# Halving the first load of a ten-stage fp32 kernel and splitting its last two projection blocks by tokens

## The chip, the cores and the metric

The kernel runs on one core of one Trainium2 chip. The metric is the device time of one execution in microseconds (us), the median over the runs shown. A core has five engines that work side by side, each through its own list of instructions in order: TensorE (PE, matrix products), VectorE (DVE), ScalarE (ACT), GpSimd (POOL) and SyncE (SP, which here only issues transfers). They wait for one another by semaphores. Transfers between the large memory (HBM) and the on-chip memory are issued by SP or by POOL, and all of them run on the core's 16 DMA engines.

## What is computed

Two models in a row on one sequence `x` of 256 tokens with 1024 features, all in float32. The first has two layers, each a mixer of three attention kinds (block attention, compressed and windowed attention, gated linear attention) followed by a feed-forward layer with a short convolution. The second has two layers, each with a feed-forward layer, a mixer (a short convolution in the first, a gated delta rule in the second) and another feed-forward layer. The end of the second model is what matters for the last part of the change:

```python
def second_block(x, norm_g, ...):
    h = x
    for i in range(DEPTH):
        g = norm_g[i]
        ff = swiglu(rms_norm_2(h, g[0]), ffn_w_gate_up[i, 0], ffn_w_down[i, 0])
        h = h + 0.5 * rms_norm_2(ff, g[1])
        ...
        ff = swiglu(rms_norm_2(h, g[4]), ffn_w_gate_up[i, 1], ffn_w_down[i, 1])
        h = h + 0.5 * rms_norm_2(ff, g[5])
    return h

def swiglu(x, w_gate_up, w_down):
    gate, up = jnp.split(x @ w_gate_up, 2, axis=-1)
    return (jax.nn.silu(gate) * up) @ w_down
```

So the last thing computed is a product with `w_down`, its norm over the 1024 features of each token, a gain, and the sum with `h`.

## The kernel before

**Stages.** `stage_list` gives ten stages: HYBRID, FFN1, HYBRID, FFN1, then FFN2, SHORT, FFN2, FFN2, DELTA, FFN2. `x` stays on the chip for the whole run, as `x[128, 2, 1024]`: 128 partitions, two chunks of 128 tokens, 1024 features. Its four quarters of 512 columns (`quarter(q)`: chunk `q % 2`, column half `q // 2`) are what a stage updates.

**Weights.** All weights come as panels of 128 x 1024 floats (512 KB), one per step, in the order of use, into a ring of six buffers `raw` (`RING = 6`). A product of float32 numbers is made of three products of rounded parts (`mm3`). So each panel is split on the chip: ACT writes the rounded part `whi` (`hi`, L991), DVE the rest `wlo = raw - whi` (`lo`, L1537), and PE waits for `lo_done`. SP reloads a ring buffer when `lo_done` says that it has been read.

**Start.** SP issues the masks, the whole of `x`, the column constants `cols` and the first six panels. PE runs ten products of a matrix of ones (L2969) and then waits for `x`. `turn_x` transposes `x` in eight tiles of 128 features and five groups (`TURNS = ((0,), (1,), (2, 3), (4, 5), (6, 7))`) into PSUM; ACT scales each tile and writes `xhi` (L1007), DVE writes `xlo` (L1548). ACT puts the split of panel 0 behind tile 1, and DVE does the same. Then `up` (L2321) multiplies panel 0, and so on. ACT also squares `x` for the norm.

**POOL at the start.** It waits for the masks and for the whole of `x` (L869), and then issues the setup loads of the hybrid stage: six constants (L882) and four small weights, `w1_in` (2 MB), `w2_in`, `pos_in` and `gate_w_in` (L887), counted by `small_loaded`. PE waits for the six before the small table product at L2491, ahead of tile 3.

**DVE's order at the start.** It is written out by hand: splits of panels and reads of tiles take turns. After its read of tile 1 DVE waits for `small_loaded` (L1823) and copies the tile into the input of the compression (L1827, L1829). Behind that in its list is the split of panel 5.

**End.** In the last stage (FFN2) each block of 128 hidden features has two `up` panels and one `down` panel. `down` (L2373) adds `h.T @ w_down` into four banks, one for each quarter, for all 256 tokens; it runs two blocks behind (`LAG = 2`), so two `down` blocks stand at the end. `finish` on ACT (L1021) squares the four banks with a running sum per token as each is complete, then takes one root for both chunks. `finish` on DVE (L1563) multiplies each bank by the gain (L1576), adds the two column halves' sums (L1573), takes the reciprocal (L1579) and makes four updates `x = gained * rstd + x` (L1591). SP waits for all four and stores `x` with one transfer of 1 MB (L857 to L859).

Of the kernel before, what the change touches and what calls it, by code (L numbers as in the profile page):

```python
# [4 lines left out]
P = 128  # L5
D = 1024
S = 256
KT = D // P
# [293 lines left out]
def build(nc, stages, arrays):  # L302
# [14 lines left out]
    with ExitStack() as ctx:  # L317
# [7 lines left out]
        HALF = D // 2  # L325
        QUARTERS = 2 * CHUNKS

        def quarter(q):
# [203 lines left out]
        def mixed(k):  # L532
# [16 lines left out]
            "consts table_product table stored rel_loaded small_loaded tile_read tok_read "  # L549
            "gla_gained squared qk_ms qk_root qk_scaled qk_turned nsa_ready moba_ready gains low_tanh gsum cmp_x "  # L550
            "cmp_hidden cmp_bias cmp_act cmp_kv vc_copied o_cmp s_sum t_ready p_ready p_scaled gated "
# [9 lines left out]
            "l16_sum l16 l32_sum l32 t32 l64_sum l64 new_sum new v1_in o_sum o_copied o_squared o_added o_root o_inv o_scaled o_turned").split()}  # L561
        x_loaded = sem("x_loaded")
        cols_loaded = sem("cols_loaded")
        landed = [sem(f"landed{i}") for i in range(RING)]
# [123 lines left out]
        def wait_x(eng, s, q):  # L688

            if s == 0:  # L690
                eng.wait_ge(x_loaded, 16)
            else:
                eng.wait_ge(x_updated, QUARTERS * (s - 1) + q + 1)

# [83 lines left out]
        def _(sp):  # L778
            sp.dma_start(masks[:], masks_in).then_inc(masks_loaded, 16)
            sp.dma_start(x[:], x_in).then_inc(x_loaded, 16)  # L780
            sp.dma_start(cols[:], cols_in).then_inc(cols_loaded, 16)
            for j in range(RING):
                sp.dma_start(raw[j][:], panels[j]).then_inc(landed[j], 16)
# [72 lines left out]

            sp.wait_ge(x_updated, QUARTERS * n_stages)  # L857
            sp.dma_start(out, x[:]).then_inc(stored, 16)
            sp.wait_ge(stored, 16)  # L859


        @block.gpsimd
        def _(pool):
# [4 lines left out]
            pool.wait_ge(masks_loaded, 16)  # L868
            pool.wait_ge(x_loaded, 16)  # L869
            def hybrid(s):  # L870
# [110 lines left out]
        def _(act):  # L981
# [16 lines left out]
            def prepare(s):  # L998

                for k in range(KT):  # L1000
                    g, src = turned(s, k)
                    if k == TURNS[g][0]:
                        act.wait_ge(x_turned, len(TURNS) * s + g + 1)
                    if s == 0 and k == 2:

                        hi_to(0)
                    act.activation(xhi[:, k, :], src, ACT.Copy, scale=col(("pre", s), k)).then_inc(xhi_ready, 1)  # L1007
                hi_to(1)
                if posts_before(s):
                    act.wait_ge(post_squared, QUARTERS * posts_before(s))  # L1010
                for c in range(CHUNKS):
                    wait_x(act, s, QUARTERS - CHUNKS + c if s and post_norm(s - 1) else QUARTERS - 1)
                    if s or c:
                        act.wait_ge(sum_ready, CHUNKS * s + c)
                    act.activation(psq[:, :, :].rearrange("p a b -> p (a b)"), x[:, c, :], ACT.Square,
                                   accum_out=row_sums[:, c:c + 1]).then_inc(sum_ready, 1)
                act.wait_ge(sum_ready, CHUNKS * (s + 1))
                act.activation(row_root[:], row_sums[:], ACT.Sqrt, scale=1.0 / D, bias=eps_col[:, 0:1]) \
                    .then_inc(root_ready, 1)

            def finish(s):  # L1021

                act.activation(root_of_one[:, s:s + 1], ones[:, 0:1], ACT.Sqrt)
                if not post_norm(s):
                    return
                n = posts_before(s)
                for q in range(QUARTERS):
                    wait_acc(act, s, q)
                    if q >= 2:
                        act.wait_ge(post_squared, QUARTERS * n + q - 1)  # L1030
                    act.activation(psq[:, q % 2, :], bank[q][:], ACT.Square, accum_out=post_parts[:, q:q + 1]) \
                        .then_inc(post_squared, 1)
                act.wait_ge(post_sum_ready, n + 1)
                half = 4.0 if stages[s][0] == FFN2 else 1.0
                act.activation(post_root[:], post_sum[:], ACT.Sqrt, scale=half / D,
                               bias=eps_col[:, 1:2] if half == 4.0 else eps_col[:, 0:1]).then_inc(post_root_ready, 1)
                hi_to(down_panel(s, n_blocks(s) - 1) + LEAD + 1)
# [60 lines left out]
            def hybrid(s):  # L1098
# [19 lines left out]
                def nsa_heads_ready():  # L1118

                    v("qk_turned", 0, 2)  # L1120
                    v("gains", 1, 2)
                    for i in range(4):
                        last = act.activation(qkn[:, i, :], bank[2 + i // 2][:, i % 2 * S:(i % 2 + 1) * S], ACT.Copy,
                                              scale=qk_gain[:, i:i + 1])
                    last.then_inc(y["nsa_ready"], 1)
# [397 lines left out]
        def _(dve):  # L1523
# [33 lines left out]
            def copy_rstd(s):  # L1557
# [3 lines left out]
                dve.wait_ge(rstd_ready, s + 1)  # L1561

            def finish(s):  # L1563
                n = posts_before(s)
                if post_norm(s):
# [160 lines left out]
            def hybrid(s):  # L1726
# [5 lines left out]
                def start():  # L1732

                    if n == 0:
                        link(dve.tensor_reduce(quarters[:], ident.rearrange("p (g j) -> p j g", g=4), AX.X, ALU.add))
                    g = col_at[("qk_gain", s)]
                    dve.tensor_copy(qk_gain[:], cols[:, g:g + 8]).then_inc(y["gains"], 1)
                    v("gains", 0, 2)
                    dve.tensor_scalar(qk_gain[:, 2:6], cols[:, g + 2:g + 6], -(HD ** -0.5), None, ALU.mult) \
                        .then_inc(y["gains"], 1)  # L1740

                    dve.tensor_scalar(gla_gain[:], col(("gla_gain", s)), 0.5, None, ALU.mult) \
                        .then_inc(y["gla_gained"], 1)

# [93 lines left out]
                def step(k):  # L1838
# [10 lines left out]
                    if k == 1:  # L1849
                        v("cmp_hidden", 1, 2)  # L1850
                        dve.tensor_copy(cmp_small[:, 0:1], bank[7][:, NCMP:NCMP + 1]).then_inc(y["cmp_bias"], 1)
                        v("gains", 1, 2)
                        v("qk_turned", 1, 2)
# [117 lines left out]
                    if k == OUT_SLOT + 3:  # L1971
                        v("gla_gained", 0, 1)
                        v("sgate", 0, 1)
# [324 lines left out]
            for k in range(KT):  # L2298
                if k == 2:
                    lo_to(0)  # L2300
                prepare_tile(0, k)
# [12 lines left out]
        def _(pe):  # L2314
# [24 lines left out]
            def turn_x(s):  # L2339
# [9 lines left out]
                for g, ks in enumerate(TURNS):  # L2349
# [9 lines left out]
                    for k in ks:  # L2359
                        dst = turned(s, k)[1]  # L2360
                        for c in range(CHUNKS):
                            last = pe.transpose(dst[:, c * P:(c + 1) * P], x[:, c, k * P:(k + 1) * P], ident)  # L2362
                    last.then_inc(x_turned, 1)

            def spread_rstd(s):
# [7 lines left out]
            def down(s, f, p, turn):  # L2373
# [5 lines left out]
                for q in range(QUARTERS):  # L2379
# [4 lines left out]
                    if q < QUARTERS - 1 and ends:  # L2384

                        last.then_inc(acc_ready, 1)
                last.then_inc(panel_used, 1)

            def blocks_of(s):
                kind = stages[s][0]  # L2390
                def body(f, turn):
# [31 lines left out]
                    if f >= LAG:  # L2423
                        down(s, f - LAG, down_panel(s, f - LAG), turn)
                run_blocks(pe, s, body)
                for f in range(n_blocks(s) - LAG, n_blocks(s)):
                    down(s, f, down_panel(s, f), None)
# [567 lines left out]
```

## Time and profile before

| | us |
|---|---|
| median of 3 runs | 1993.9 |
| the three runs | 1993.9, 1994.35, 1991.03 |
| span of the profiled execution (first to last instruction) | 1991.5 |
| PE busy | 1961.4 (98%) |
| DVE busy | 1398.7 (70%) |
| ACT busy | 1095.4 (55%) |
| POOL busy | 125.0 (6%) |
| mean DMA throughput | 175 GB/s |
| mean granted clock of PE, share of full | 0.995 |

The profiled execution has no time of its own beside its span; the runs' median lies 2.4 us above that span. A busy share is the share of the span in which the engine had an instruction under way. Matrix products overlap, so the distance between two starts says more than the duration of one. An idle time in brackets stands with what ended it.

### The profile page before, as it was taken

To read this page: it belongs to the slowest core of one execution; us is meant where nothing else is said; L and a number is where in the kernel's file an instruction comes from. 1 tells how busy PE (TensorE), PEld (TensorE's weight loads), DVE (VectorE), ACT (ScalarE), POOL (GpSimd) and SP (SyncE) were. 2 spreads that over 40 slices of the span, in tenths; PEclk is the share of its full clock that TensorE was granted. 3 is DMA by queue.
4 is the path that set the end of the run, shared out by engine and by line. 5 is a ranking of instruction groups with operands and counts; after the bars stand their busy time and mean duration, and the time that the engine had idled before them with its cause. 6 is when DMAs were issued, how large, how long until landed. Compare 5 with 4: busy or idle time off the path is not lost.

```text
span 1991.5 us, 41716 instructions
## 1 busy us (share of the span) xinstructions
PE 1961.4 (98%) x15682; PEld 1827.6 (92%) x15682; DVE 1398.7 (70%) x2392; ACT 1095.4 (55%) x1828; POOL 125.0 (6%) x204
## 2 busy tenths in 40 slices
PE   9999999999999999999999999999999899999998
PEld 7999999989999999999999999999999899989997
DVE  6687877766788877666667766666658977577655
ACT  5665555556654655554454544454447777565443
POOL 2031000000040000000000000000000432000000
PEclk9999999999999999999999999999999899999999
DMA  9433665554335555465546465555554535455552
GB/s 319 143 128 128 217 210 189 187 170 149 128 118 190 200 187 186 156 212 189 190 159 212 151 202 187 189 174 187 188 190 150 164 123 155 149 173 195 188 187 82
DMA packets 117817, 348.51 MB, mean 175 GB/s; under 512 B 23288, under 2 KB 35912, under 8 KB 117184
## 3 DMA queue, kind: packets, MB, share of 16 engines
q1 hardware_dynamic: 114960, 335.23, 50.6%
q0 software_dynamic: 2736, 11.59, 1.7%
q8 instruction: 85, 1.39, 0.3%
q14 instruction: 36, 0.29, 0.1%
HBM read 340.81 MB, written 5.96 MB: 174 GB/s over the span
## 4 chain that ended last, share of the span: by engine, by line
PE 90%; DVE 4%; ACT 2%; issue 1%; DMA 1%; POOL 1%; SPq 0%; DVEq 0%; ACTq 0%; POOLq 0%
PE bank L2317 28%; PE bank L2319 27%; PE bank L2318 27%; PE bank L2609 1%; ACT whi L991 1%; DVE arena L1576 1%; DVE wlo L1537 1%; DVE conv L2038 1%; PE bank L2353 1%; PE bank L2582 0%; DMA relay<-arena 0%; PE bank L2796 0%; PE bank L2570 0%; PE bank L2362 0%; DVE xlo L1548 0%
## 5 line engine op out<-in xcount | busy, mean ns | idle before, releaser
L2317 PE MATMUL bank<-xhi,whi 128*128 128x256 f32 x3368 | 958.4, 285 | 7.3 <-DVE arena L2031 2.6
L2318 PE MATMUL bank<-xlo,whi 128*128 128x256 f32 x3368 | 943.9, 280 | 1.1 <-issue 1.1
L2319 PE MATMUL bank<-xhi,wlo 128*128 128x256 f32 x3368 | 943.2, 280 | 1.1 <-issue 1.1
L1537 DVE TENSOR_TENSOR wlo<-raw,whi 128x1024 fp32r<-128x1024 f32 x621 | 750.1, 1230 | 199.6 <-ACT whi L991 196.9
L2317 PEld LDWEIGHTS bank<-xhi,whi 128*128 128x128 f32 x3368 | 635.7, 189 | 24.3 <-issue 6.1
L2318 PEld LDWEIGHTS bank<-xlo,whi 128*128 128x128 f32 x3368 | 636.2, 189 | 5.8
L991 ACT ACTIVATE whi<-raw 128x1024 fp32r<-128x1024 f32 x621 | 632.2, 1045 | 11.9 <-DMA raw<-panels 6.2
L2319 PEld LDWEIGHTS bank<-xhi,wlo 128*128 128x128 f32 x3368 | 635.8, 189 | 1.2 <-issue 1.2
L2317 PE MATMUL bank<-whi,hhi 128*128 128x512 f32 x688 | 272.8, 396 | 0.0
L2319 PE MATMUL bank<-whi,hlo 128*128 128x512 f32 x688 | 271.2, 394 | 0.0
L2318 PE MATMUL bank<-wlo,hhi 128*128 128x512 f32 x688 | 270.4, 393 | 0.0
L1048 ACT ACTIVATE act_out<-first 128x256 f32<-128x256 f32 x89 | 37.3, 419 | 301.9 <-DVE first L1662 301.7
L1662 DVE TENSOR_TENSOR first<-bank,rstd 128x256 f32<-128x256 f32 x132 | 56.0, 424 | 184.8 <-PE bank L2319 184.6
L1070 ACT ACTIVATE hhi<-h 128x256 fp32r<-128x256 f32 x172 | 71.9, 418 | 185.5 <-PE bank L2319 125.6
L2319 PEld LDWEIGHTS bank<-whi,hlo 128*128 128x128 f32 x688 | 129.4, 188 | 29.9
L2318 PEld LDWEIGHTS bank<-wlo,hhi 128*128 128x128 f32 x688 | 130.1, 189 | 23.5
L2317 PEld LDWEIGHTS bank<-whi,hhi 128*128 128x128 f32 x688 | 129.3, 188 | 23.4
L1055 ACT ACTIVATE conv<-first,cols 128x256 f32<-128x256 f32 x44 | 26.5, 603 | 126.6 <-DVE first L1662 126.6
L1699 DVE TENSOR_TENSOR hlo<-h,hhi 128x256 fp32r<-128x256 f32 x172 | 71.9, 418 | 24.0 <-ACT hhi L1070 19.3
L1693 DVE TENSOR_TENSOR h<-act_out,second 128x256 f32<-128x256 f32 x132 | 55.8, 423 | 22.3 <-ACT act_out L1061 22.3
L1161 ACT ACTIVATE arena<-arena 128x256 f32<-128x256 f32 x48 | 20.0, 417 | 70.2 <-DVE arena L1819 70.2
L932 POOL DMA_DIRECT2D arena<-gains_in x6 | 3.3, 550 | 850.4 <-DVE arena L1576 721.3
(376 smaller groups left out, 1751.8 us busy)
## 6 DMA issues: line engine op xcount, KB each, us to landing
raw<-panels SPq DMA_DIRECT2D x621, 512.0 KB, 3.8
arena<-w_in POOLq DMA_DIRECT2D x2, 2048.0 KB, 10.5
arena<-relay SPq DMA_DIRECT2D x8, 512.0 KB, 5.0
arena<-gains_in POOLq DMA_DIRECT2D x6, 512.0 KB, 3.9
relay<-arena POOLq DMA_DIRECT2D x4, 512.0 KB, 9.1
relay<-arena SPq DMA_DIRECT2D x4, 512.0 KB, 3.6
x<-x_in SPq DMA_DIRECT2D x1, 1024.0 KB, 5.0
arena<-bias_table POOLq DMA_DIRECT2D x8, 128.0 KB, 6.5
```

The source lines that it names most:

```text
L991: act.activation(whi[slot][:], raw[slot][:], ACT.Copy).then_inc(hi_done, 1)
L1048: act.activation(act_out[:, sl, :], first[:, sl, 2:], ACT.Silu).then_inc(act_done, 1)
L1055: act.activation(conv[:, sl, :], first[:, sl, 2:], ACT.Identity, scale=tap(s, 2, f, turn), bias=conv_bias(s, f, turn)) \
L1070: act.activation(hhi[:, sl, :], h[:, sl, :], ACT.Copy).then_inc(hhi_done, 1)
L1161: act.activation(g, g, ACT.Tanh, scale=0.5).then_inc(y["merged"], 1)
L1537: dve.tensor_tensor(wlo[slot][:], raw[slot][:], whi[slot][:].bitcast(F32), ALU.subtract) \
L1662: dve.tensor_tensor(first[:, sl, 2:], pair[:, 0:S], rstd[:], ALU.mult).then_inc(gate_scaled, 1)
L1693: dve.tensor_tensor(h[:, sl, :], gated, second[:, sl, :], ALU.mult).then_inc(h_done, 1)
L1699: dve.tensor_tensor(hlo[:, sl, :], h[:, sl, :], hhi[:, sl, :].bitcast(F32), ALU.subtract) \
L2317: pe.matmul(dst, w_hi, a_hi, start=start, stop=False, skip_group_check=True)
L2318: pe.matmul(dst, w_hi, a_lo, start=False, stop=False, skip_group_check=True)
L2319: return pe.matmul(dst, w_lo, a_hi, start=False, stop=stop, skip_group_check=True)
```

## The change

It has five parts.

1. `x` is loaded in two halves of 512 columns: masks, first half, `cols`, panel 0, second half, panels 1 to 5. Whoever needs tiles 0 to 3 waits for the first half, everyone else, POOL's first wait among them, for the second.
2. In the first stage PE issues products of ones between the groups of transposes: 1, 1, 6, 2 and 2 of them behind the five groups.
3. ACT and DVE split panel 0 behind tile 3 in place of tile 1.
4. The last two `down` blocks of the last stage are done first for tokens 0 to 127 and then for tokens 128 to 255. The banks are complete in the order 0, 2, 1, 3. Square, sum, root, reciprocal and update are done for each chunk of tokens by itself, and each quarter of `x` is stored by a transfer of its own.
5. The semaphore `gla_gained` is merged into `gains`, whose count per hybrid stage goes from 2 to 3.

```diff
+        LAST_ORDER = (0, 2, 1, 3)
...
+        x_second_half_loaded = sem("x_second_half_loaded")
...
         def wait_x(eng, s, q):
             if s == 0:
-                eng.wait_ge(x_loaded, 16)
+                eng.wait_ge(x_loaded if q < CHUNKS else x_second_half_loaded, 16)
...
         def _(sp):
             sp.dma_start(masks[:], masks_in).then_inc(masks_loaded, 16)
-            sp.dma_start(x[:], x_in).then_inc(x_loaded, 16)
+            sp.dma_start(x[:, :, 0:HALF], x_in[:, :, 0:HALF]).then_inc(x_loaded, 16)
             sp.dma_start(cols[:], cols_in).then_inc(cols_loaded, 16)
-            for j in range(RING):
+            sp.dma_start(raw[0][:], panels[0]).then_inc(landed[0], 16)
+            sp.dma_start(x[:, :, HALF:], x_in[:, :, HALF:]).then_inc(x_second_half_loaded, 16)
+            for j in range(1, RING):
                 sp.dma_start(raw[j][:], panels[j]).then_inc(landed[j], 16)
...
-            sp.wait_ge(x_updated, QUARTERS * n_stages)
-            sp.dma_start(out, x[:]).then_inc(stored, 16)
-            sp.wait_ge(stored, 16)
+            for i, q in enumerate(LAST_ORDER):
+                c, j = quarter(q)
+                sp.wait_ge(x_updated, QUARTERS * (n_stages - 1) + i + 1)
+                sp.dma_start(out[:, c, j * HALF:(j + 1) * HALF], x_quarter(q)).then_inc(stored, 16)
+            sp.wait_ge(stored, 16 * QUARTERS)
...
             pool.wait_ge(masks_loaded, 16)
-            pool.wait_ge(x_loaded, 16)
+            pool.wait_ge(x_second_half_loaded, 16)
...
-                    if s == 0 and k == 2:
+                    if s == 0 and k == KT // 2:
                         hi_to(0)
...
+                if s == n_stages - 1:
+                    for i, q in enumerate(LAST_ORDER):
+                        wait_acc(act, s, i)
+                        if i >= 2:
+                            act.wait_ge(post_squared, QUARTERS * n + i - 1)
+                        act.activation(psq[:, i % 2, :], bank[q][:], ACT.Square, accum_out=post_parts[:, q:q + 1]) \
+                            .then_inc(post_squared, 1)
+                        if i % 2:
+                            c = i // 2
+                            act.wait_ge(post_sum_ready, n + 1 + c)
+                            act.activation(post_root[:, c:c + 1], post_sum[:, c:c + 1], ACT.Sqrt, scale=4.0 / D,
+                                           bias=eps_col[:, 1:2]).then_inc(post_root_ready, 1)
+                    return
...
+            def finish_last(s):
+                n = posts_before(s)
+
+                def weighted(i):
+                    q = LAST_ORDER[i]
+                    dve.wait_ge(post_squared, QUARTERS * n + i + 1)
+                    dve.tensor_tensor(gained[:, q, :], bank[q][:], gain[:, q // CHUNKS * HALF:(q // CHUNKS + 1) * HALF],
+                                      ALU.mult).then_inc(post_gained, 1)
+
+                dve.wait_ge(gain_loaded, 16 * (n + 1))
+                for c in range(CHUNKS):
+                    cs = slice(c, c + 1)
+                    weighted(2 * c)
+                    dve.wait_ge(post_squared, QUARTERS * n + 2 * c + 2)
+                    dve.tensor_tensor(post_sum[:, cs], post_parts[:, cs], post_parts[:, CHUNKS + c:CHUNKS + c + 1], ALU.add) \
+                        .then_inc(post_sum_ready, 1)
+                    weighted(2 * c + 1)
+                    dve.wait_ge(post_root_ready, n + 1 + c)
+                    dve.reciprocal(post_rstd[:, cs], post_root[:, cs]).then_inc(post_rstd_ready, 1)
+                    dve.wait_ge(post_rstd_ready, 3 * n + 1 + c)
+                    for i in (2 * c, 2 * c + 1):
+                        q = LAST_ORDER[i]
+                        dve.wait_ge(post_gained, QUARTERS * n + i + 1)
+                        dve.scalar_tensor_tensor(out=x_quarter(q), in0=gained[:, q, :], scalar=post_rstd[:, cs],
+                                                 in1=x_quarter(q), op0=ALU.mult, op1=ALU.add).then_inc(x_updated, 1)
...
-                if k == 2:
+                if k == KT // 2:
                     lo_to(0)
                 prepare_tile(0, k)
...
                     last.then_inc(x_turned, 1)
+                    if s == 0:
+                        for i in range(6 if ks[-1] == KT // 2 - 1 else len(ks)):
+                            pe.matmul(bank[2][:, 0:P], ones[:], ones[:], start=True, stop=True)
...
+            def last_downs(s):
+
+                nb = n_blocks(s)
+                for c in range(CHUNKS):
+                    ts = slice(c * P, (c + 1) * P)
+                    for f in (nb - 2, nb - 1):
+                        p = down_panel(s, f)
+                        slot, sl = p % RING, f % 2
+                        pe.wait_ge(lo_done, used(p))
+                        pe.wait_ge(hlo_done, first_block[s] + f + 1)
+                        for j in range(2):
+                            q, cs = CHUNKS * j + c, slice(j * HALF, (j + 1) * HALF)
+                            last = mm3(bank[q][:], hhi[:, sl, ts], hlo[:, sl, ts], whi[slot][:, cs], wlo[slot][:, cs],
+                                       False, f == nb - 1)
+                            if f == nb - 1 and q != LAST_ORDER[-1]:
+                                last.then_inc(acc_ready, 1)
+                        if c == CHUNKS - 1:
+                            last.then_inc(panel_used, 1)
...
                 run_blocks(pe, s, body)
+                if s == n_stages - 1:
+                    last_downs(s)
+                    return
                 for f in range(n_blocks(s) - LAG, n_blocks(s)):
                     down(s, f, down_panel(s, f), None)
```

## Rows read from the trace of the kernel before

**Rows 1.** The page: PE's busy time, and the chain that ended last.
```profile
PE 1961.4 (98%) x15682; PEld 1827.6 (92%) x15682; DVE 1398.7 (70%) x2392; ACT 1095.4 (55%) x1828; POOL 125.0 (6%) x204
...
PE 90%; DVE 4%; ACT 2%; issue 1%; DMA 1%; POOL 1%; SPq 0%; DVEq 0%; ACTq 0%; POOLq 0%
```

**Rows 2.** Timeline, first 12 us: start, duration, engine and line, operation, [idle before].
```profile
6.32 1.94 PE L2362 MATMUL bank<-masks,x 128*128 128x128 f32 x16 [1.04 <-DMA x<-x_in]
...
6.83 0.67 POOL L882 DMA_DIRECT2D rel_table<-rel_in  x1 [5.76 <-DMA x<-x_in]
...
8.15 1.06 ACT L991 ACTIVATE whi<-raw 128x1024 fp32r<-128x1024 f32 x1 [0.48 <-DMA raw<-panels]
...
10.52 0.39 PE L2317 MATMUL bank<-xhi,whi 128*128 128x256 f32 x1 [2.27 <-DVE wlo L1537]
...
11.74 0.52 POOL L887 DMA_DIRECT2D arena<-gate_w_in  x1
```

**Rows 3.** DMA issues up to 34 us: size, and us from issue to landing.
```profile
arena<-w_in POOLq DMA_DIRECT2D x1, 2048.0 KB, 12.9
x<-x_in SPq DMA_DIRECT2D x1, 1024.0 KB, 5.0
...
arena<-gate_w_in POOLq DMA_DIRECT2D x1, 16.0 KB, 13.8
```

**Rows 4.** Timeline of DVE, 25 to 28 us.
```profile
25.57 0.66 DVE L1827 COPY arena<-tmp 128x240 f32<-128x240 f32 x2 [4.74 <-DMA arena<-gate_w_in]
...
26.23 1.22 DVE L1537 TENSOR_TENSOR wlo<-raw,whi 128x1024 fp32r<-128x1024 f32 x1
```

**Rows 5.** Timeline of PE's weight loads, 27.2 to 28 us: the first of panel 5.
```profile
27.50 0.19 PEld L2317 LDWEIGHTS bank<-whi,xhi 128*128 128x128 f32 x1 [0.23 <-DVE wlo L1537]
```

**Rows 6.** Timeline of all engines, from 1977 us to the end.
```profile
1977.82 0.43 DVE L1699 TENSOR_TENSOR hlo<-h,hhi 128x256 fp32r<-128x256 f32 x1 [1.85 <-ACT hhi L1070]
...
1979.91 0.39 PE L2317 MATMUL bank<-whi,hhi 128*128 128x512 f32 x1
...
1981.59 2.02 DVE L1576 TENSOR_TENSOR arena<-bank,arena 128x512 f32<-128x512 f32 x3 [3.34 <-ACT psq L1031]
...
1982.46 0.39 PE L2319 MATMUL bank<-whi,hlo 128*128 128x512 f32 x1
...
1982.89 0.60 ACT L1031 ACTIVATE psq<-bank 128x512 f32<-128x512 f32 x1
...
1983.61 0.16 DVE L1573 TENSOR_TENSOR post_sum<-post_parts 128x2 f32<-128x2 f32 x1
...
1983.81 0.30 ACT L1035 ACTIVATE post_root<-post_sum,eps_col 128x2 f32<-128x2 f32 x1 [0.23 <-DVE post_sum L1573]
1984.29 0.16 DVE L1579 RECIPROCAL post_rstd<-post_root 128x2 f32<-128x2 f32 x1
1984.48 2.74 DVE L1591 SCALAR_TENSOR_TENSOR x<-arena,post_rstd,x 128x512 f32<-128x512 f32 x4
1987.25 0.34 SPq L858 DMA_DIRECT2D out<-x  x1
```

**Rows 7.** DMA issues at the end, and all panel loads up to 40 us.
```profile
out<-x SPq DMA_DIRECT2D x1, 1024.0 KB, 3.9
...
DMA to landing us min/median/max: 3.2/8.5/12.0
```

**Rows 8.** Three windows: busy (x count) of PE, PEld, DVE, ACT, POOL; granted clock; DMA share; GB/s.
```profile
12.00:15.00 3.00, 3.00 (x17) 3.00 (x16) 1.98 (x5) 2.88 (x7) 1.25 (x3) 0.52 1.02 406
1568.00:1572.00 4.00, 0.22 (x2) 0.01 (x1) 3.96 (x12) 3.93 (x10) 0.00 (x0) 0.92 0.72 200
1572.00:1582.00 10.00, 9.63 (x251) 9.05 (x252) 8.31 (x19) 6.00 (x9) 0.00 (x0) 0.52 0.71 237
```

**Rows 9.** DMA queues, 16 to 22 us and 22 to 25 us (q0: POOL's, q1: SP's).
```profile
q0 software_dynamic: 144, 2.03, 80.1%
...
q1 hardware_dynamic: 281, 1.02, 87.8%
```

More of the change, by code:

```diff
@@ L549, in build @@
             "consts table_product table stored rel_loaded small_loaded tile_read tok_read "
-            "gla_gained squared qk_ms qk_root qk_scaled qk_turned nsa_ready moba_ready gains low_tanh gsum cmp_x "
+            "squared qk_ms qk_root qk_scaled qk_turned nsa_ready moba_ready gains low_tanh gsum cmp_x "
             "cmp_hidden cmp_bias cmp_act cmp_kv vc_copied o_cmp s_sum t_ready p_ready p_scaled gated "
@@ L1011, in prepare @@
                 for c in range(CHUNKS):
+                    if s == 0:
+                        wait_x(act, s, 0)
                     wait_x(act, s, QUARTERS - CHUNKS + c if s and post_norm(s - 1) else QUARTERS - 1)
@@ L1120, in nsa_heads_ready @@
                     v("qk_turned", 0, 2)
-                    v("gains", 1, 2)
+                    v("gains", 1, 3)
                     for i in range(4):
@@ L1561, in copy_rstd @@
                 dve.wait_ge(rstd_ready, s + 1)
+            def finish_last(s):
[21 more added lines that the diff above has]
+                                                 in1=x_quarter(q), op0=ALU.mult, op1=ALU.add).then_inc(x_updated, 1)
             def finish(s):
+                if s == n_stages - 1:
+                    finish_last(s)
+                    return
                 n = posts_before(s)
@@ L1737, in start @@
                     dve.tensor_copy(qk_gain[:], cols[:, g:g + 8]).then_inc(y["gains"], 1)
-                    v("gains", 0, 2)
+                    v("gains", 0, 3)
                     dve.tensor_scalar(qk_gain[:, 2:6], cols[:, g + 2:g + 6], -(HD ** -0.5), None, ALU.mult) \
@@ L1742, in start @@
                     dve.tensor_scalar(gla_gain[:], col(("gla_gain", s)), 0.5, None, ALU.mult) \
-                        .then_inc(y["gla_gained"], 1)
+                        .then_inc(y["gains"], 1)
                 def heads_mean(i, at, n_heads):
@@ L1851, in step @@
                         dve.tensor_copy(cmp_small[:, 0:1], bank[7][:, NCMP:NCMP + 1]).then_inc(y["cmp_bias"], 1)
-                        v("gains", 1, 2)
+                        v("gains", 1, 3)
                         v("qk_turned", 1, 2)
@@ L1971, in step @@
                     if k == OUT_SLOT + 3:
-                        v("gla_gained", 0, 1)
+                        v("gains", 2, 3)
                         v("sgate", 0, 1)
@@ L2363, in turn_x @@
                     last.then_inc(x_turned, 1)
+                    if s == 0:
+                        for i in range(6 if ks[-1] == KT // 2 - 1 else len(ks)):
+                            pe.matmul(bank[2][:, 0:P], ones[:], ones[:], start=True, stop=True)
             def spread_rstd(s):
@@ L2425, in blocks_of @@
                 run_blocks(pe, s, body)
+                if s == n_stages - 1:
+                    last_downs(s)
+                    return
                 for f in range(n_blocks(s) - LAG, n_blocks(s)):
```

## The prediction

> **What bounds the kernel now.** I read the page first: TensorE (PE) is busy for 98% of the span [rows 1], so almost everything is one queue of products, and a change moves the time only where PE waits, or before its first and after its last product. So I read next the timeline of the first 12 us, the DMA landings and waits up to 34 us, and the timeline from 1977 us on.
>
> In the front [rows 2] the reader is to see that the transposes start at 6.32, when the whole input has landed (issued at 1.22, 5.0 us to landing [rows 3]), and that the first product starts at 10.52, after ACT and DVE have split panel 0 (its load landed by 8.15). But the front does not end there. VectorE (DVE) sits idle 4.74 us ahead of L1827, until 25.57, for four small-weight loads of the GpSimd queue (`small_loaded`) [rows 4]. The last is `gate_w_in`, issued at 11.74 and landed 13.8 us later, at 25.54 [rows 2, 3]. Behind this wait on DVE's queue stands the split of panel 5 (26.23 to 27.45) [rows 4], and PE's first weight load of panel 5 starts at 27.50, released by that very split [rows 5]. So **two paths meet at 27.5**: PE's own work, and GpSimd's load, then DVE. PE had stalled there for at most 0.2 us.
>
> At the end [rows 6], PE's last block is 12 products, 1979.91 to 1982.46, 0.232 us apart, the last one done at 1982.85. Then come: the square (1982.89, 0.70 with its read), the sum (1983.61), the root (1983.81 to 1984.11), the reciprocal (1984.29), four updates (1984.48 to 1987.22), and one 1 MB store, issued at 1987.25 and landed 3.9 us later at 1991.15 [rows 7]. That is 8.3 us behind PE's last product, with everything in series.
>
> **The front, part by part.** (a) Halving the input. The SP queue's loads land in the order of issue: masks, input, columns, panels. The first half then has 0.5 MB fewer bytes ahead of its end; at 0.41 MB per us, the rate of 12 to 15 us [rows 8], it lands about 1.2 us earlier, near 5.0. The transposes of tiles 0 to 3 can follow the ten warm-up products at once (these end at 5.27, the 1.04 us before 6.32), ScalarE can begin near 5.7 and is free for panel 0, which lands near 6.9, when it has scaled four tiles. I put panel 0's split ready at about 10.1 in place of 10.5: 0.4 us. (b) The 12 added ones products cost 0.22 us each at full clock (two passes of 128 columns), some 2.7 us; eight stand between the first three turns and the second half's arrival, where PE would wait in any case, the other four in the 2.27 us that PE now idles before 10.52 [rows 2]. Cost nothing; if that cover is gone, 0.9 us. What they can give: from 12 to 15 us the granted clock is 0.52 of full [rows 8], the 1.2 GHz level, after that idle time; full clock there is worth about 1.6 us. So PE would arrive at panel 5 about 2.0 us earlier. (c) One more SP issue (0.42 us) is ahead of panels 1 to 5 and delays none that is awaited. (d) **GpSimd's wait moves.** It stood on the whole input, at 6.2; it now stands on the second half, which is issued behind panel 0. The bytes ahead of its end are those ahead of panel 0's end now, so it lands near 8.1: 1.9 us later. Queued behind the wait are all ten setup loads, `gate_w_in` last. Are they shifted one for one? The first was issued at 6.83 [rows 2]. While `w1_in` moves, the GpSimd queue has 80% of the DMA engines' time; in 22 to 25, when the last small ones move, SP's queue has 88% [rows 9]. SP's panels keep a backlog throughout: what it moves early in those 1.9 us it has fewer later, but 5.2 MB for panels 1 to 10 at 0.41 MB per us, with GpSimd's 2.9 MB (2 MB of them `w1_in` [rows 3]) beside it, fill the engines until about 27.5. So no hole opens for the shifted loads to catch up in. I take 1.9 us; the ends are 0 (they catch up wholly) and 2.2.
>
> So `small_loaded` comes at 27.4, DVE's two copies and panel 5's split end at 29.35 (the same 1.9 us as from 25.54 to 27.45), and PE starts panel 5 at 29.4 in place of 27.5. The 2.0 us that (a) and (b) give are spent waiting there: **the front loses 1.9 us.** The small-table product at L2491 waits for the first six loads, at 17.0 now, 18.9 then, when PE reaches it at about 19.2: nothing. POOL's table store follows panel 5 and is not near a bound.
>
> (e) PE then idles from about 25.6 to 29.4. After 2.27 us idle it was granted half clock at 12 to 15; after the 4 us around 1568 to 1572 (busy 0.22) the next 10 us were at 0.52 [rows 8]. So I expect half clock again on panels 5 and 6. In the first case it began about 3.2 us after the idle time did and lasted to about 14.8; put from 25.6 on, it lies over 29.4 to 31.9 and costs half of that, 1.2 us. The ends are 0 and 4.8 (the 10 us stretch). The Trainium skill (TensorE: Matmul & The Clock Gate, Part 1) says that an idle array falls back to 1.2 GHz; by that rule, the trace agrees.
>
> After panel 5 PE is the bound: the chain that ended last lies on it for 90% [rows 1], and the squares and turns that follow start from panel 5's end. The shift passes to the end one for one. The merge of `gla_gained` into `gains` changes no order of work: nothing.
>
> **The tail.** `last_downs` has the same 24 products, in another order. Its block 20 begins near 1977.1 (12 products ahead of 1979.91) and has six products for tokens 0 to 127, so needed at 1978.5 is `hlo` of the last block, ready at 1978.25 [rows 6]: cover 0.25 us; if it is gone, the difference is lost. Bank 0 is whole at 1979.4, bank 2 at 1980.1, bank 1 at 1982.15, bank 3 at 1982.85 as now. For tokens 0 to 127: squares 1979.4 to 1980.8; gain products of 0.68 [rows 6] from 1980.2; sum by 1981.05; root by 1981.4; reciprocal 1981.8; two updates of 0.685, to 1983.2. All this lies beside PE or after it. DVE is now the bound for the other tokens: gain product of bank 1 to 1983.9, sum 1984.05, gain product of bank 3 to 1984.65 (the root, 1984.1 to 1984.4, beside it), reciprocal 1984.8, updates to 1985.5 and 1986.2. In place of 1987.22: **1.0 us.** Late next is DVE's queue, as the sum waits 0.3 us for it.
>
> The last store has 256 KB in place of 1 MB; three go before it, 0.7 us apart or more, so they have drained. The price of such a store is in no row: below stands 3.9 less the 0.79 MB that it has fewer, at 0.41 MB per us, 2.0; above, the fastest 512 KB panel load, 3.2 [rows 7]. I take 2.3, near the first because that is the same kind of transfer: 1.6 us saved, between 0.7 and 1.9. [...] **The tail gains 2.6 us.**
>
> **Sum:** 1.9 + 1.2 - 2.6 = +0.5 us on the profiled execution, 1991.5 to 1992.0. The median of the three runs is 1993.9, 2.4 above that span, so the forecast is 1994.4 us. A measurement of this kernel can tell about 0.2%, 4 us, from no change; the three runs lie 3.3 us apart.
>
> **Rivals.** A (forecast, chance 0.5): as above. B, the GpSimd loads catch up (0.2): DVE's wait ends at 25.5 as now, the front neither gains nor loses, the tail gives 2.6: 1991.3. For it: in 16 to 22 its queue has 80% of the DMA time, so it is hardly slowed by SP. Against it: the last small loads crawl beside SP's 88% [rows 9]. C, DVE's wait is no gate and PE's lead survives (0.1): -2.0 - 2.6 gives 1989.3. Against it is the load at 27.50, released by the split [rows 5]. D, the slower side (0.1): the idle time ahead of panel 5 brings the long half-clock stretch, as after 1572. Its place is panels 5 to 8, its price 4.8 in place of 1.2, and it decides if the stretch outlasts panel 6: 1998.0. E, the tail gives nearly nothing (0.1): PE stalls in `last_downs` by the lost cover, and the store costs 3.2: 1994.4 + 1.2, 1995.6. The change not doing what it says would be that the ones products do not hold the clock in the first two tiles: nothing in the time under A, since PE waits at panel 5.
>
> **How the numbers follow.** The likeliest is A's 1994.4. The range takes in B, E and D's edge, with the spread of the three runs about A: 1990.4 to 1997.9. Faster by over 0.2% means below 1989.9: most of C and the edge of B, 0.09. Slower means above 1997.9: half of D and the edge of A, 0.08. The rest is 0.83.
>
> **What would show it.** GpSimd's first setup load issued near 8.7; L1827 on DVE near 27.4 after over 6 us idle; PE's wait ahead of panel 5 of 3 us or more, with half clock after it; the last update ending 3.4 us after PE's last product, in place of 4.4; the last store landing about 2.3 us after its issue. L1827 at 25.6 would make (d) wrong; a start of panel 5 before 27.5 would make the whole front wrong.

## The result, and the profile after

The changed kernel takes **1996.12 us** in the median of 21 runs (1991.76 to 2000.4), the kernel before 1993.57 us in 21 runs beside it (1989.88 to 1996.29). The ratio is 1.0015, 95% interval [1.0009, 1.0021]: about 3 us slower, inside the 0.2% that the prediction called no change, and inside its range. The profile is of the fastest of the 21 runs: its span is 1990.0 us, 1.5 *under* that of the profile before. So the profile alone would say the opposite of the median, and what lies between them became the question of the experiments.

PE's line of the page, which answers to [rows 1]:

```profile
PE 1963.5 (99%) x15706; PEld 1829.0 (92%) x15706; DVE 1398.2 (70%) x2394; ACT 1096.2 (55%) x1829; POOL 124.6 (6%) x204
```

PE has 24 products and 24 weight loads more: the twelve products of ones, two passes each. The 48 matter further down.

**The front.** Timeline of the changed kernel, answering to [rows 2] and [rows 4] (L2412 is the transposes, L2417 the added ones, L888 GpSimd's first setup load, L1877 DVE's copy behind the small weights, L1558 the splits):

```profile
6.04 0.41 PE L2412 MATMUL bank<-masks,x 128*128 128x128 f32 x2 [0.34 <-DMA x<-x_in]
...
10.04 0.63 PE L2412 MATMUL bank<-masks,x 128*128 128x128 f32 x4 [1.15 <-DMA x<-x_in]
...
10.54 0.68 POOL L888 DMA_DIRECT2D rel_table<-rel_in  x1 [9.47 <-DMA x<-x_in]
...
13.07 0.39 PE L2367 MATMUL bank<-xhi,whi 128*128 128x256 f32 x1 [1.07 <-DVE wlo L1558]
...
27.09 0.66 DVE L1877 COPY arena<-tmp 128x240 f32<-128x240 f32 x2 [4.59 <-DMA arena<-gate_w_in]
...
27.75 1.22 DVE L1558 TENSOR_TENSOR wlo<-raw,whi 128x1024 fp32r<-128x1024 f32 x1
...
29.02 0.50 PE L2367 MATMUL bank<-whi,xhi 128*128 128x512 f32 x1 [0.31 <-DVE wlo L1558]
```

The first half of `x` lands at 6.0, hardly before the whole did (6.2), as it took 4.7 us from its issue and the whole 5.0; the second lands at 9.9. The first product starts at 13.07 in place of 10.52. The first two of the following rows are DMA issues of the changed kernel (both halves with their median, then the second half alone); the two behind them are the window from 2 to 4 us, of the kernel after and before, whose last column is GB/s:

```profile
x<-x_in SPq DMA_DIRECT2D x2, 512.0 KB, 5.8
...
x<-x_in SPq DMA_DIRECT2D x1, 512.0 KB, 6.8
...
2.00:4.00 2.00, 2.00 (x11) 2.00 (x11) 0.00 (x0) 0.25 (x2) 0.00 (x0) 1.00 0.61 170
```

```profile
2.00:4.00 2.00, 2.00 (x11) 2.00 (x11) 0.00 (x0) 0.24 (x2) 0.00 (x0) 1.00 0.99 304
```

From 2 to 4 us the 16 DMA engines are busy for 61% in place of 99% and move 170 GB/s in place of 304. All the traces of this document divide so: in the seven with the halved load the rate is 155 to 190 GB/s, in the seven with the whole one 297 to 319. The half of `x` goes as 256 rows of 2 KB in place of 128 of 8 KB, and its issue occupies SP for 0.69 us in place of 0.42. Some 0.27 MB are lost there, and everything behind is late. For all that, `gate_w_in` lands only 1.5 us later than before (11.6 us after an issue at 15.47, in place of 13.8 after 11.74), and PE starts panel 5 at 29.02 in place of 27.5. PE does not wait at panel 5 for long (0.31 us, its weight load 0.75), as it comes late itself. There is no half clock in the front: behind the warm-up products the granted clock is 1.00 up to 1572 us.

**The end**, answering to [rows 6] and [rows 7]:

```profile
1983.99 0.40 PE L2369 MATMUL bank<-whi,hlo 128*128 128x512 f32 x1
...
1984.54 0.68 DVE L1590 TENSOR_TENSOR arena<-bank,arena 128x512 f32<-128x512 f32 x1
...
1985.15 0.16 DVE L1598 TENSOR_TENSOR post_sum<-post_parts 128x1 f32<-128x1 f32 x1
1985.22 0.68 DVE L1590 TENSOR_TENSOR arena<-bank,arena 128x512 f32<-128x512 f32 x1
...
1985.82 0.15 DVE L1602 RECIPROCAL post_rstd<-post_root 128x1 f32<-128x1 f32 x1
1986.01 1.41 DVE L1607 SCALAR_TENSOR_TENSOR x<-arena,post_rstd,x 128x512 f32<-128x512 f32 x2
...
out<-x SPq DMA_DIRECT2D x4, 256.0 KB, 2.1
```

DVE is never idle here for longer than 0.1 us. The last update ends 3.0 us behind PE's last product (4.4 before), and a store of 256 KB lands in 2.1 us.

**Between front and end.** ACT runs one small root at the end of each of the ten stages, so that line splits the span. Before (L1023) and after (L1031):

```profile
L1023 ACT ACTIVATE root_of_one<-ones x10: 186/203/203, 235.4 to 1979.1; 128x1 f32<-128x1 f32 x10
```

```profile
L1031 ACT ACTIVATE root_of_one<-ones x10: 188/203/205, 236.9 to 1980.6; 128x1 f32<-128x1 f32 x10
```

The first stage is 1.5 us longer, the piece behind the last root 3.1 shorter (12.4 and 9.3), and all the others agree within 0.1 us in this pair. (Over all fourteen profiles of this document, every stage but the first and the ninth agrees within 0.2 us.) The ninth, the delta stage, hides something. It lies from 1504 to 1791 us here. PE's waits in it that no semaphore explains, which the profile puts down to "issue", are, in the window 1640 to 1680 us, before and after:

```profile
PE bank L2319 <- issue: 1.1, 1, 1.1
```

```profile
PE bank L2902 <- issue: 3.6, 1, 3.6
```

and its timeline after:

```profile
1655.77 0.68 PE L2902 MATMUL bank<-arena 32*16 32x16 f32 x59
1660.03 0.21 PE L2902 MATMUL bank<-arena 32*16 32x16 f32 x3 [3.59 <-issue]
```

PE stands for 3.6 us three products short of the end of a run of small ones (32 rows, 16 columns, two operations of the list for each product), which it works off at about 11 ns each. I counted PE's operations (weight loads, products, its own waits) from 5 us ahead of the stage: the long wait falls at operation 3839, and a shorter one at 2559. Before, waits of 1.1 us fall at 3887 and 2607, and one of 1.6 at 4911, for which the changed kernel has no counterpart. The two in each kernel lie 1280 apart, five times 256 (the third another 1024, four times 256), and the pairs lie 48 apart: the 48 operations that the products of ones add in front. The page's queue q8, "instruction", moved 1.39 MB in 85 transfers, 16 KB each. From this came theory F: PE's list is fetched in blocks of 256, and a block whose end falls in a run of very short products, or right behind one, is awaited longest. The Trainium skill (Runtime: NRT & Kernel Launch, Terms) has the engines' instruction memory refilled in blocks of 16 KiB, and (Perfetto Trace Analysis, The 4-stage abstract model) an instruction of 64 bytes; 16 KiB by 64 bytes is 256, an estimate from both, and the traces agree.

### The profile page after: what moved, and what is told of

It is laid out like the page before. It is cut to its first block, busy times and chain, and to the rows that moved or that the text cites. A ratio compares the mean times of both kernels' runs of the same rounds, so it can differ in the third digit from the quotient of the medians.

```text
span 1990.0 us, 41775 instructions
## 1 busy us (share of the span) xinstructions
PE 1963.5 (99%) x15706; PEld 1829.0 (92%) x15706; DVE 1398.2 (70%) x2394; ACT 1096.2 (55%) x1829; POOL 124.6 (6%) x204
## 3 DMA queue, kind: packets, MB, share of 16 engines
q8 instruction: 85, 1.39, 0.3%
## 4 chain that ended last, share of the span: by engine, by line
PE 91%; DVE 3%; ACT 2%; DMA 2%; POOL 1%; issue 1%; SPq 0%; DVEq 0%; ACTq 0%; POOLq 0%
PE bank L2367 28%; PE bank L2369 27%; PE bank L2368 27%; PE bank L2685 1%; ACT whi L997 1%; DVE arena L1626 1%; DVE wlo L1558 1%; DMA arena<-gate_w_in 1%; PE bank L2403 1%; PE bank L2872 0%; PE bank L2658 0%; PE bank L2646 0%; PE bank L2412 0%; POOL arena L978 0%; DVE xlo L1569 0%
## 5 line engine op out<-in xcount | busy, mean ns | idle before, releaser
L1558 DVE TENSOR_TENSOR wlo<-raw,whi 128x1024 fp32r<-128x1024 f32 x621 | 749.8, 1230 | 201.1 <-ACT whi L997 198.4
```

Of the source, the lines that this page charges most:

```text
L1558: dve.tensor_tensor(wlo[slot][:], raw[slot][:], whi[slot][:].bitcast(F32), ALU.subtract) \
```

## The experiments

Times are medians; each ratio is to the kernel before, run beside it. A change of 0.001 is 2 us. The three numbers behind a run are, from its profile, the first stage, the delta stage and the piece behind the last root (before: 235.4, 287.4 and 12.4 us; after: 236.9, 287.3 and 9.3).

**The end alone**, everything else as before:

> The kernel before with the change's end alone: last two down blocks by token halves, norm per half, four stores. Theory G (the end gains, the front loses through GpSimd's late setup loads): 3.0 us faster than the kernel before, as the profile after shows 5.6 us from PE's last product to the end of the span in place of 8.6; the front as before (DVE's wait for small_loaded ends near 25.5). Rival T (the end is what made the change slower, by a wait that the one profile does not show): no gain or a loss.

Measured: 1988.5 us, ratio 0.9981 [0.9971, 0.9991]; 235.5, 287.8, 9.3. And once more, with other kernels beside it:

> The end alone once more, beside the variants of this call: 3.1 us under the kernel before by the length of the last piece of the span (9.3 in place of 12.4 us), and not the 3.8 of the first measurement of nine runs.

Measured: 1989.27 us, 0.9984 [0.9975, 0.9993]; 235.5, 286.0, 9.3. The end gives its 3 us; rival T falls.

The second profile also shows the gate at panel 5 [rows 5] at work. Its granted clock was 1.00 from 12 to 16 us, with no added products, where the kernel before has 0.64. So PE came to panel 5 earlier, its weight load waited 0.89 us there in place of 0.23, and the first stage was no shorter:

```profile
27.57 0.19 PEld L2363 LDWEIGHTS bank<-whi,xhi 128*128 128x128 f32 x1 [0.89 <-DVE wlo L1554]
```

**The front alone** (the end undone):

> The change with its end undone: halved load, ones products, panel 0 split later, GpSimd's wait on the second half. Theory G: slower than the kernel before by 2.6 + 3.0 = 5 to 6 us, which the front of the profile after (1.5 us) shows only in part; this profile should show DVE's wait for small_loaded ending later than 27.1, or half clock behind PE's idle time ahead of panel 5. Rival T: within 1 us of the kernel before.

Measured: 1998.18 us, 1.0026 [1.0015, 1.0036]; 237.9, 287.1, 12.4. It costs 5 us, of which this profile, again of one of the fastest runs, shows half, in the first stage. T falls a second time. DVE's wait ended at 28.0, and PE's weight load waited 1.89 us for panel 5, in place of 0.75 in the profile of the change with the same front:

```profile
29.92 0.19 PEld L2349 LDWEIGHTS bank<-whi,xhi 128*128 128x128 f32 x1 [1.89 <-DVE wlo L1543]
```

So what GpSimd's moved wait costs differs from run to run.

**GpSimd waits for the first half:**

```diff
-            pool.wait_ge(x_second_half_loaded, 16)
+            pool.wait_ge(x_loaded, 16)
```

> The change, but GpSimd waits for the first half of x only, so its ten setup loads are issued from about 6.6 us on, as in the kernel before. Theory G: DVE's wait for small_loaded ends near 25.5 again and the time falls by what the front lost: 3 to 5 us under the change, 1 to 3 us under the kernel before. Rival L (the slow loads of 2 KB rows and PE's late start at panel 0, 13.1 in place of 10.5, are the loss, and GpSimd's wait is not): no different from the change.

Measured: 1994.2 us, 1.0007 [0.9999, 1.0016]; 236.4, 290.2, 9.3. DVE's wait ended at 25.3, as theory G has it, and the first stage is 0.5 us shorter: the moved wait is real, but by these profiles a small part. The median is some 1.5 us under the change, with intervals that overlap; G's 3 to 5 us are not there.

**The change again:**

> The changed kernel itself, for a second profile, since the first is of the fastest of its 21 runs. Theory G: 2 to 3 us over the kernel before in the median; in the profile the first stage is longer than the 236.9 us of the first profile, by 2 to 4 us, and all the stages between as before. Rival N (nothing in the front; the spread lies in a later stage): stage one at 236.9 and a later stage longer.

Measured: 1995.91 us, 1.0012 [1.0003, 1.0021]; 236.7, 292.4, 9.3. The first stage is as in the first profile; **the delta stage is 5 us longer.** That is rival N. The stalls are at 2559 and 3839 again, 2.1 and 3.6 us, with a third of 1.1 us at 1535, and the clock is at half from 1574 for 6.8 us, from 1615 for 6.8 and from 1663 for 6.8; in the change's first profile it was from 1572 for 10.2 and from 1661 for 3.4. Theory F was formed here.

**Forty-eight operations and nothing else**, in the kernel before:

```diff
             for i in range(10):
                 pe.matmul(bank[2][:, 0:P], ones[:], ones[:], start=True, stop=True)
+            for i in range(12):
+                pe.matmul(bank[2][:, 0:8], ones[:], ones[:, 0:8], start=True, stop=True)
             pe.wait_ge(masks_loaded, 16)
```

> The kernel before with twelve more products of ones, 8 columns each, behind the ten warm-up products, where PE waits 1.0 us for x. They add 48 instructions to PE's list, as the change's twelve do, and nothing else. Theory F (PE's instructions are fetched in blocks of 256; 48 more in front move a block's end into the delta rule's run of small products, and PE stands there without instructions): the delta stage shows the long stall at instruction 3839 of the stage, 3.6 us in place of 1.1 at 3887, as all four traces of the changed front do, and the time is 2 to 5 us over the kernel before, with a front longer by at most 0.5 us. Rival G (the loss is the late loads in the front): no stall of over 1.5 us there, and within 0.5 us of the kernel before.

Measured: 1997.67 us, 1.0023 [1.0011, 1.0036]; 237.2, 290.8, 12.4. The stall moved to operation 3839 and became 3.6 us, with nothing of the change's loads, waits or end in the kernel:

```profile
PE bank L2826 <- issue: 3.6, 1, 3.6
```

The padding was dearer than I wrote: it took 2.95 us where PE waited 1.0, and 1.8 us of the 4.6 are in the first stage, for a forecast of 0.5 at most. The other 2.8, or 3.4 by the two profiles' delta stages, are what is left for theory F. These are seven runs, from 1990.5 to 2000.5 us.

**The change without its products of ones** (the loop in `turn_x` is out):

> The change without its twelve products of ones. Theory F: the block ends fall where they did before (stalls at 2607 and 3887, of about 1.1 us), the delta stage is 3 to 5 us shorter than in the typical run of the change, and the median is 3 to 4 us under the change; half clock in the front may take back up to 1.6 us. Rival G: no different from the change, or slower by the half clock alone.

Measured: 1993.49 us, 1.0005 [0.9996, 1.0014]; 238.9, 286.7, 9.3. The stalls are back at 2607 and 3887, of 1.1 and 0.8 us. The front is 2.0 us longer than with the ones: the granted clock is 0.50 from 12 to 16 us, where it was 1.00 with them.

```profile
12.00:16.00 4.00, 2.71 (x12) 2.71 (x13) 3.93 (x6) 3.89 (x8) 4.00 (x8) 0.50 1.04 397
```

So the ones do hold the clock: none of the eight traces with ones behind the turns has half clock in the front, and five of the six without them have (the end alone, measured again, is the sixth). What they give in the front their 48 operations take back, with interest, 1600 us later: without them the median is 2 us nearer to the kernel before, though the front is 2.0 us longer.

**The same, and GpSimd on the first half:**

> The change without its products of ones and with GpSimd waiting for the first half only. Theory F and G together: below g2 by 0.5 to 1.5 us, since DVE's wait for the small weights is gone from the front; the best of the variants that keep the halved load, near 1990 us. If only G held: as the earlier run with GpSimd on the first half, 1994.2 us.

Measured: 1994.26 us, 1.0008 [0.9999, 1.0017]; 239.7, 290.5, 9.3. A miss: no gain over the run before it. Its clock was at half in the front for 10.2 us, from 9 on, and in the delta stage for 10.2 us from 1586. Its stalls at 2607 and 3887 are short (0.5 and 0.8 us), but there is one of 2.1 us at 1583, another 1024 before 2607, which ends at 1585.2, just ahead of that half clock. So where the blocks end does not alone set the delta stage's length: with the same ends a wait can come or stay away.

**The change with `x` loaded whole** (ones, the order of the splits and the end kept):

> The change with x loaded whole and GpSimd waiting for it as in the kernel before; the products of ones, the later split of panel 0 and the end as in the change. Theory F: the stall at 3839 stays, so the median is within 2 us of the change (front 1.4 us shorter at most). Theory L (the halved load with 2 KB rows is what costs the front): the first stage takes 235.4 us or less in place of 236.8.

Measured: 1994.69 us, 1.0013 [1.0004, 1.0022]; 235.8, 290.1, 9.3. The halved load with its moved wait costs the first stage 1.0 us, by profiles. The stalls are at 2559 (2.2 us) and 3839 (1.1), with one of 0.7 us at 1535, and the median stays near the change, as F has it.

**The same cover in 12 operations.** Products of 384 columns cover as much time with a quarter of the list. In the change:

```diff
-                        for i in range(6 if ks[-1] == KT // 2 - 1 else len(ks)):
-                            pe.matmul(bank[2][:, 0:P], ones[:], ones[:], start=True, stop=True)
+                        for i in range({KT // 2 - 1: 2, KT - 1: 1}.get(ks[-1], 0)):
+                            pe.matmul(bank[2][:, 0:3 * P], ones[:], masks.rearrange("p a b -> p (a b)"),
+                                      start=True, stop=True)
```

> The change with its twelve products of 128 columns replaced by three of 384, two ahead of the second half and one behind the last turn: about the same time under cover, 12 instructions in place of 48. Theory F: the first stage as in the change (236.9 us), no stall at 3839 in the delta stage, which takes 286.5 to 288 us in a typical run; median 2.5 to 3.5 us under the change, about 1 us under the kernel before. Rival: the median stays at the change's.

Measured: 1992.03 us, 0.9996 [0.9987, 1.0005]; 236.8, 287.4, 9.3. The first stage is the change's, the stalls are at 3875 and 2595, of 1.6 and 1.8 us, and the median is over 3 us under the change. Together with the padded kernel this shows that the number of operations counts, not what they do.

The traces say more on theory F than these pairs. In the delta stages of all fourteen PE has 43 waits of over 0.35 us that no semaphore explains, up to 3.8 us long. By the count above, every one falls at the same remainder by 256 within a kernel: 47 where PE's list is as long as before, 35 where it has 12 operations more, 255 where it has 48 more. Every one ends 2.2 to 2.6 us after a 16 KB transfer of the instruction queue has started. In this stage that queue makes 25 transfers in every trace, and PE works off 6421 operations, 25.1 times 256. So the fetch in blocks of 256 is shown. Why one block comes late and another in time is not; that short products use a block up too fast is argued from where the longest waits fall.

**The end, with wide ones and `x` loaded whole** (the kernel before with the change's end, and three products of 384 columns behind the last turn):

> The same without moving DVE's wait. Theory G (in the kernel before, panel 5 is released by DVE behind its wait for the small weights, so whatever the front saves ahead of it is lost there): first stage 235.4 us as in the kernel before, and the time that of the end alone. Rival: first stage shorter by the 1.6 us of half clock that the products save.

Measured: 1989.91 us, 0.9986 [0.9977, 0.9995]; 235.8, 287.7, 9.4. The clock stays full in the front, and PE loses what that gives at panel 5, for which its weight load now waits 1.30 us in place of 0.23 [rows 5]:

```profile
27.85 0.19 PEld L2363 LDWEIGHTS bank<-whi,xhi 128*128 128x128 f32 x1 [1.30 <-DVE wlo L1554]
```

**And DVE's wait moved behind panel 6's split** (in the first hybrid stage L1823 to L1829 run ahead of tile 4):

```diff
-                    if t == 1:
+                    if t == 1 and n:
+                        compression_input()
...
                 def before(t):
+                    if t == 4 and n == 0:
+                        compression_input()
```

> The kernel before with the change's end, three products of ones with 384 columns behind the last turn (12 instructions in place of the change's 48, about 1.9 us of cover), x loaded whole, and in the first hybrid stage DVE's wait for the small weights and its copies moved behind the split of panel 6. Theory F and G together: the delta stage keeps its stalls of 1.1 us, since a shift of 12 instructions does not reach the run of small products; the first half clock is gone and panel 5 no longer waits, so the first stage takes 233.5 to 234 us in place of 235.4 and the median is 1 to 2 us under the end alone: the best of all. Rival: the first stage stays at 235.4, as something else starts panel 5.

Measured: 1988.62 us, 0.9983 [0.9974, 0.9992]; 235.1, 286.6, 9.3. PE runs through panel 5 without a wait, but only 0.3 to 0.7 us of the 1.4 to 1.9 expected come out, set against the first stages of the kernel before (235.4), the end alone (235.5) and the run above (235.8). In this run the transposes started 0.4 us later than in the run above (6.84, not 6.46), as `x` landed later, and PE arrived at panel 5 near 27.1 by itself. Its median lies under those of the kernel before and of the change; from the end alone (1988.5, 1989.27) it cannot be told apart.

## Why the prediction was right, and where it was wrong

**The end** was right, in mechanism and nearly in size: DVE became the bound, the updates ended 1.4 us earlier in relation to PE's last product (forecast 1.0), the last store took 2.1 us (forecast 2.3), 3.1 us in all for 2.6. The two runs of the end alone give 3.2 and 3.8. (Rival E was priced wrongly: 1.2 us over the forecast leaves the end 1.4 of its 2.6 us, not "nearly nothing".)

**Step (a), the halved load, was wrong.** It put the first half at 5.0, the second at 8.1 and panel 0's split ready at 10.1. Measured were 6.0, 9.9 and 13.07. It took the DMA rate of 12 to 15 us, 0.41 MB per us, for the first 4 us, where the whole load moved 304 GB/s and the halved one 170, so it also missed that the half in rows of 2 KB would be the slower one.

**Step (d), GpSimd's wait,** was right in place and in effect, wrong in both of its sizes, which nearly cancelled: its loads were issued 3.7 us later, not 1.9, but they did catch up by half (11.6 us to landing in place of 13.8), so DVE's wait ended at 27.09 for a forecast of 27.4. That it is the cause of the front's loss was the failing inference. PE reached panel 5 late by itself and its weight load waited 0.75 us; with the wait taken back (25.3) the first stage fell by only 0.5 us. The front alone, with 1.89 us of wait, shows that it can cost more. The gate at panel 5 is real in the kernel before, as the end with wide ones and the second run of the end alone show: 1.30 and 0.89 us of wait in place of a shorter first stage.

**Step (e)** forecast 3.8 us of idle time and 1.2 us of half clock at panel 5. (By its own readings, 25.6 and the 6.6 us from 8.25 to 14.86, the stretch would have ended at 32.2 and cost 1.4.) Neither came. The 1.9 + 1.2 us of the front were 1.5 in the first profile, 1.3 in the second, and 2.5 in that of the front alone.

**"Cost nothing" for the twelve products, step (b), is the step that failed.** It counted their time and not their place in PE's list. They hold the clock as said (2.0 us of the first stage with the halved load), and by moving the ends of the fetched blocks they cost some 3 to 4 us in the delta stage. Between the change and its twin with 12 operations lie 3.8 us by the ratios (3.0 over the kernel before, 0.8 under it; the two intervals do not meet), and 2.8 are left in the padded kernel before.

The medians can be read together. From each run's difference to the kernel before (by its ratio) I take what its first stage and its end differ, by its profile. What is left, an estimate, is 2.7 to 5.3 us in the six runs with 48 operations more (4.6 and 4.2 in the two of the change), and -0.8 to +0.9 in the seven with none or 12 more; each of these has about 2 us to either side, but the two groups lie apart. The profiles' delta stages say the same less clearly: the six profiles with 48 more have a mean of 289.7 us (287.1 to 292.4), the eight with none or 12 more 287.5 (286.0 to 290.5).

How the moved blocks cost time shows in part. Near 1615 and 1660 us PE waits 5.3 us in the mean of the six, 2.2 in that of the eight. The granted clock is 0.50 there for 3.4 to 13.7 us in each of the six, and in one of the eight (3.4 us), so a part of the price is half clock about the waits. Against this, the eight wait 1.6 us in the mean near 1697, and the six do not. How much of the 3 to 4 us each of these makes is not settled.

**The sum** then reads +1.5 (front) - 3.1 (end) + 3.6 (delta stage, the mean of what is left in the four other runs with 48 more) = +2.0, for a measured +3.0 by the ratio, with an interval of +1.8 to +4.2. **That the forecast of +0.5 came out inside its range was luck:** a loss of 3 to 4 us, 1600 us behind the front, stood in no term and no rival, and of the 3.1 us forecast for the front only 1.5 came. The signs named for the front's loss, 3 us or more of wait at panel 5 and half clock behind it, were not there. What remains is not settled: the delta stage is up to 5 us longer in one run than in another of the same kernel, with its half-clock stretches, and a profile is one draw of it.

## What to carry to other kernels

Products put in to hold TensorE's clock should be few and wide. Under cover they cost nothing where they run, but here they cost where they shifted the fetch of the list, and a run of very short products far behind is where to look (waits put down to "issue"). Ahead of an engine's wait for a late load put all that does not need the load; a saving ahead of a gate is lost at the gate. And where a kernel's runs spread by 8 us, no single profile, least of all that of the fastest run, explains a median that moved by 3.

## What the runs showed that I had not expected

- PE's list of operations is fetched in blocks of 256: all 43 waits for it in the delta stages of fourteen traces fall at one remainder within a kernel. Moving it by 48 with products of 8 columns made a wait of 1.1 us into one of 3.6, and with all it brought the kernel before from 1992.3 to 1997.7 us.
- Those products of 8 columns were not cheap: 24 passes took 2.95 us, and from 6 us on, at a granted clock of 1.00, they started 0.11 us apart, as far as the changed kernel's passes of 128 columns do.
- Halving a load of 1 MB into two of 512 KB whose rows fall from 8 to 2 KB left the DMA engines idle for 39% of the time from 2 to 4 us, and the first half landed only 0.2 us before the whole had.
